# Query-key products of the second block from fp32r halves: three products in place of one full fp32 product

## The chip, the cores and the metric

The kernel runs on one core of one Trainium2 chip. The metric is the device time in microseconds (us) of one execution; lower is better. The core has five engines that matter here: PE (TensorE, matrix products), ACT (ScalarE), DVE (VectorE), POOL (GpSimd) and SP, which only issues the loads of weights. Each works through its own queue in order and waits on semaphores for the others.

## The reference

The whole computation is a model of two blocks on a sequence of 512 tokens and width 1024, all in fp32. The first block (a pooling layer, a dilated attention layer and two convolutional feed-forward layers) is not touched. The second block has two layers; each projects the normed input to seven parts and runs four "retention" heads and four "stick-breaking" heads of width 128, then an output projection and a gated feed-forward layer. What the change touches are the products of queries and keys of both kinds of head:

```
scores = jnp.einsum('bhnid,bhnjd->bhnij', qc, kc) * intra_decay[:, None]      # retention, q and k rotated
intra = jnp.einsum('bhnij,bhnje->bhnie', scores, vc)
...
z = jnp.einsum('bhtd,bhsd->bhts', qb, kb).astype(jnp.float32) * scale         # stick-breaking
valid = s_pos < t_pos
log_keep = jnp.where(valid, jax.nn.log_sigmoid(-z), 0.0)
later = lax.cumsum(log_keep, axis=3, reverse=True) - log_keep
w = jnp.where(valid, jnp.exp(jax.nn.log_sigmoid(z) + later), 0.0)
```

## The kernel before

Most matrix products of the kernel are made of fp32r halves. A value is split into a high half (ACT writes it, as a copy into an fp32r tile) and a low half (DVE subtracts the high half from the value, into another fp32r tile), and a product is then three: high by high, low by high, high by low (three(), called by gemm()). A few products still take fp32 operands whole, and among them are the keys by queries of the second block: products(), called by r1() for a retention head and by s1() for a stick-breaking head. For one head a set of products is four products, one for each block of 128 keys, that are 512, 384, 256 and 128 columns wide (only keys up to the query count); 1280 columns in all. The profile records a full fp32 product as two matmul instructions.

In each of the two layers, eight tiles of value weights come first, then 20 tiles for the heads: five for each of four head pairs x = 0 to 3, in phases ph = 0 to 4: the stick-breaking keys, its queries, the retention keys, its queries, and the gate. One tile is a gemm() of 24 matmuls. Head work is laced into this stream of tiles by hand, at fixed places on each engine:

- PE, loop over t in pe_program. For pair x: s3 of the pair before (weights by values, stick-breaking) in phase 0 after k = 3; r1 of the pair before ahead of phase 1; finish(x-1, 0), the two products that sum a head's squares for its norm, in the middle of phase 1; r2 of the pair before ahead of phase 2; in the middle of phase 2 first finish(x-1, 1) and then s1(x); in phase 4 after k = 1 the cumulative sums s2(x). After the last pair s3, r1, and then the output projection (group()), with the last finish and r2 inside.
- ACT, loop over t in act_program. prep() copies a tile of weights to its high half, two tiles ahead. In phase 2: r2 (copy of a head's output and its square), finish (Ln and Exp of the norm), s1 for the two narrow blocks (Abs, Exp, Ln), head_high, turned_pair (two copies TMP that swap the halves of the rotated keys, as soon as the tile of phase 2 is done), s1 for the two wide blocks. In phase 3 s1_high makes SPH, the high half for s2.
- DVE, loop in dve_program. prep() makes the low halves of the weights. In phase 2: square_low, finish, s1 for the narrow blocks, head_low, the rotated keys (K<-PS,RT), s1 for the wide blocks. At the head of phase 3 s1_low makes SPO, which s2 on PE reads.
- POOL multiplies TMP by the sine and adds it to K or Q. SP loads weight tiles into two RAW buffers, each after the low half of the tile that was there.

Keys and queries lie in three buffers each, K[n] and Q[n], used in turn. PE's accumulators for z are banks 2 to 4.

Of the kernel before, what the change touches and what calls it, by code (L numbers as in the profile page):

```python
# [6 lines left out]
F32 = mybir.dt.float32  # L7
# [294 lines left out]
    return n * p + sum(sets(i) for i in range(m)), (n - 4) * p + sum(sets(i) - 1 for i in range(m))  # L302


STD = {FFN1: 6, FFN2: 5, FFN3: 5}
FACTORS = {1: (((),) * 6, ((0,), (2,), (5,), (8,), (10,), ()), ((1,), (3,), (6,), (9,), (11,), ()),
               ((), (4,), (7,), (), (), ())),
# [55 lines left out]
class Core:  # L363


    def __init__(self, nc, stream, cd, colsd, xt, basd, attd, retd, out):
# [79 lines left out]
        self.G = [at(f"G{i}", 173056 + 2048 * i, 512) for i in range(2)]  # L446
        self.W = [at("WS", 177152, 2048), at("WR", 219136, 2048)]
        self.CT, self.MU = at("CT", 227328, 4), at("MU", 227392, 16)
        self.TMP = {"k": at("TMP0", 185344, 512), "q": at("TMP1", 187392, 512)}
        self.AA, self.SPL = at("AA", 189440, 1280), at("SPL", 194560, 1280)  # L450
        self.SPH, self.SPO = at("SPH", 199680, 1280, F32R), at("SPO", 204800, 1280, F32R)
# [11 lines left out]
        def sem(name):  # L463
# [2 lines left out]

        self.mix = [sem(f"mix{i}") for i in range(5)]
        self.raw, self.ara = [sem(f"raw{i}") for i in range(2)], [sem(f"ara{i}") for i in range(6)]
        self.d_c, self.d_co, self.d_bas, self.d_att, self.d_ret = (
            sem(n) for n in ("d_c", "d_co", "d_bas", "d_att", "d_ret"))  # L470
        self.d_x, self.d_out = [sem(f"d_x{i}") for i in range(4)], sem("d_out")

        self.kon, self.cond, self.ada, self.gain = sem("kon"), sem("cond"), sem("ada"), sem("gain")
# [41 lines left out]
            sem(n) for n in ("fmm", "fln", "frs", "fy", "fg", "fh", "fl"))  # L515

        self.gained, self.yd = sem("gained"), sem("yd")

        self.tv, self.th, self.tl = sem("tv"), sem("th"), sem("tl")
        self.uv, self.uh, self.ul, self.c1 = (sem(n) for n in ("uv", "uh", "ul", "c1"))  # L520
# [130 lines left out]
def pe_program(c):  # L651
# [400 lines left out]
    ffn(1, FFN1, None, (3, BANK["norm3"]))  # L1052


    def products(K, Q, order, done):

        for y in order:
            b, c0 = SBK[y]
            vacate(b)
            mm(PS[b][:, c0:c0 + WID[y]], K[:, 128 * y:128 * y + 128], Q[:, 128 * y:512],  # L1060
               y < 2 or y == (3 if order[0] else 2), True).then_inc(done, 1)

    def r1(l, x):
        h, n = 4 * l + x, (2 * x + 1) % 3
        q.wait_ge(c.rq, 2 * h + 2)
        products(c.K[n], c.Q[n], (0, 1, 2, 3), c.zr)
        for y in (0, 1, 2, 3):
            free[SBK[y][0]] = (c.rd, 4 * h + y + 1)

# [11 lines left out]

    def s1(l, x):
        h, n = 4 * l + x, 2 * x % 3
        q.wait_ge(c.sqk, 2 * h + 2)
        products(c.K[n], c.Q[n], (3, 2, 1, 0), c.zs)
        for y in (3, 2, 1, 0):
            free[SBK[y][0]] = (c.zf, 4 * h + 4 - y)

# [76 lines left out]
    for l, first, out, f, ffn0 in ((0, IN0, OUT0, 2, FFN2), (1, IN1, OUT1, 3, FFN3)):  # L1165
        value_tiles(l, first, 0)
        value_tiles(l, first + 4, 1)
        for t in range(20):
            x, ph = divmod(t, 5)
            if x and ph == 1:  # L1170
                r1(l, x - 1)
            elif x and ph == 2:
                r2(l, x - 1)

            def mid(k):
                if x and ph == 0 and k == 4:
                    s3(l, x - 1)
                elif x and ph == 1 and k == 4:
                    finish(l, x - 1, 0)
                elif ph == 2 and k == 4:  # L1180
                    if x:
                        finish(l, x - 1, 1)
                    s1(l, x)
                elif ph == 4 and k == 2:
                    s2(l, x)

            h = 4 * l + x
            freed = ((c.sqk, 2 * h + 1), (c.sqk, 2 * h + 2), (c.rot, 2 * h + 1), (c.rot, 2 * h + 2), (c.g0, h + 1))[ph]
            gemm(first + 8 + t, c.H1H, c.H1L, split(16 * l), freed, mid)
        s3(l, 3)  # L1190
        r1(l, 3)

        def mixed(k):
            return (c.fl, 8 * l + (2 * k + 2 if k < 4 else 2 * k - 7))

        def hook(n):
            if n == 3:
                finish(l, 3, 0)
                r2(l, 3)
            elif n == 8:  # L1200
                finish(l, 3, 1)

        group(out, [(c.HH, c.HL, mixed)] * 3, [(c.res, RES[out] + n + 1) for n in range(3)],
              (4, 0, 5, 1, 6, 2, 7, 3), 6, hook)
        for n in range(3, 8):
            gemm(out + n, c.HH, c.HL, mixed, (c.res, RES[out] + n + 1))
        ffn(f, ffn0, split(16 * l + 8), None, lambda k: norm(5 + 2 * l, 7) if k == 4 else None)
# [3 lines left out]
def act_program(c):  # L1211
# [108 lines left out]


    table("silu")
    nc.scalar.dma_start(c.COND[0:1, :], c.cd.rearrange("(o n) -> o n", o=1)).then_inc(c.d_c, 16)
    q.wait_ge(c.d_c, 16)
    act(c.COND[0:1, :], c.COND[0:1, :], ACT.Silu).then_inc(c.cond, 1)
    for k in range(8):
        q.wait_ge(c.d_x[k // 2], 16)
# [373 lines left out]
    def s1_high(h):  # L1701
        q.wait_ge(c.lat, 4 * h)
        for y in (3, 2, 1, 0):
            q.wait_ge(c.msk, 4 * h + 4 - y)
            act(c.SPH[:, OFF[y]:OFF[y] + WID[y]], c.SPL[:, OFF[y]:OFF[y] + WID[y]]).then_inc(c.sph, 1)

    def s2(h):
        for y in (3, 2, 1, 0):
            a = c.AA[:, OFF[y]:OFF[y] + WID[y]]
            q.wait_ge(c.laf, 4 * h + 4 - y)  # L1710
            act(a, a, ACT.Exp).then_inc(c.wex, 1)
# [56 lines left out]
    for l, first, out, f, ffn0 in ((0, IN0, OUT0, 2, FFN2), (1, IN1, OUT1, 3, FFN3)):  # L1768
# [22 lines left out]
        for t in range(20):  # L1791
            x, ph = divmod(t, 5)
            h = 4 * l + x
            if ph == 1 and x:
                gate(h - 1)
            elif ph == 3:
                s1_high(h)
            prep(first + 8 + t + 2)
            if ph == 0 and x:
                s3(h - 1)  # L1800
            elif ph == 1 and x:
                finish(h - 1, 0)
                head_high(h - 1, 0)
            elif ph == 2:
                if x:
                    r2(h - 1)
                    finish(h - 1, 1)
                s1(h, (3, 2))
                if x:
                    head_high(h - 1, 1)  # L1810
                turned_pair(t, h, 2)
                s1(h, (1, 0))
            elif ph == 3:
                turned_pair(t, h, 3)
            elif ph == 4:
                s2(h)
        prep(out + 2)
        h = 4 * l + 3
        s3(h)
        gate(h)  # L1820
        finish(h, 0)
# [33 lines left out]
def dve_program(c):  # L1855
# [523 lines left out]
    def scores(p, m):  # L2379

        u = 4 * p + m
        n, w = blocks(m)
        q.wait_ge(c.al0, 8)
        q.wait_ge(c.tr, turned(u - 1)[0] if u else 0)
        q.wait_ge(c.d_att, 16)
        for hh in range(2):
            sb = c.SB[u % 2][:, 512 * hh:512 * hh + 512]
            q.wait_ge(c.s1, 2 * u + hh + 1)
            stt(sb[:, 0:128 * n], c.ATT[:, 256 - 128 * n:256], float(SL[0][2 * p + hh]), PS[2 + hh][:, 0:128 * n],
                ALU.mult, ALU.add)  # L2390
            for g in (1, 2):
                o = 96 + 160 * g + 96 - 32 * m
                ins = stt(apart(sb, m, g), c.ATT[:, o:o + 64 * w].rearrange("p (m j) -> p m j", j=32),
                          float(SL[g][2 * p + hh]), apart(PS[2 + hh], m, g), ALU.mult, ALU.add)
            ins.then_inc(c.b4, 1)
        for hh in range(2):
            o, z = 512 * hh, 8 * (u % 2) + 4 * hh
            q.wait_ge(c.b4, 2 * u + hh + 1)
            step(nc.vector.tensor_reduce(c.STAT[:, z:z + 1], c.SB[u % 2][:, o:o + 128 * (n + w)], AX_X, ALU.max))
            nc.vector.tensor_scalar(c.STAT[:, z + 1:z + 2], c.STAT[:, z:z + 1], -1.0, None, ALU.mult  # L2400
                                    ).then_inc(c.mx, 1)
# [90 lines left out]
    def s1_low(h):  # L2492
        for y in (3, 2, 1, 0):
            o = slice(OFF[y], OFF[y] + WID[y])
            q.wait_ge(c.sph, 4 * h + 4 - y)
            tt(c.SPO[:, o], c.SPL[:, o], c.SPH[:, o].bitcast(F32), ALU.subtract).then_inc(c.spo, 1)

    def s2(h):
        def later(y):
            b, c0 = LBK[y]  # L2500
# [14 lines left out]

    def r1(h):
        q.wait_ge(c.zr, 4 * h + 4)
        q.wait_ge(c.d_ret, 16 * (h // 4 + 1))
        q.wait_ge(c.so, h + 1)
        for y in range(4):  # L2520
            b, c0 = SBK[y]
# [39 lines left out]
    for l, first, out, f, ffn0 in ((0, IN0, OUT0, 2, FFN2), (1, IN1, OUT1, 3, FFN3)):  # L2561
        for t in range(28):
            x, ph = divmod(t - 8, 5)
            h = 4 * l + x
            if t >= 8 and ph == 3:
                s1_low(h)
            prep(first + t + 2)
            if l == 0 and 2 <= t <= 9:
                stt(c.xk(t - 2), c.xk(t - 2), c.cols("final_g", t - 2), c.SS[:, :], ALU.mult, ALU.mult
                    ).then_inc(c.xs, 1)  # L2570
            if t < 8:
                if t == 1 and l == 0:
                    both()
                elif t == 5:
                    q.wait_ge(c.nrs, NORMN[7] if l else 0)
                    q.wait_ge(c.fac, 1)
                    q.wait_ge(c.d_ret, 16 * (l + 1))
                    tt(c.COS, c.COS, c.SG[:, :], ALU.mult)
                    tt(c.SIN, c.SIN, c.SG[:, :], ALU.mult).then_inc(c.turn, 1)
                elif t == 7:  # L2580
                    values_out(l, first)
                continue
            if ph == 1 and x:
                r1(h - 1)
                finish(h - 1, 0)
                head_low(h - 1, 0)
            elif ph == 2:
                if x:
                    square_low(h - 1, 1)
# [21 lines left out]
                    s1(h, (1, 0))  # L2611
            else:
                tt(c.G[h % 2][:, :], P, c.SG[:, :], ALU.mult).then_inc(c.g0, 1)
        prep(out + 2)
        h = 4 * l + 3
        square_low(h, 0)
        r1(h)
        finish(h, 0)
# [74 lines left out]
def sp_program(c):  # L2693
# [35 lines left out]
    for u in range(6, len(UNITS)):  # L2729
        load(u)  # L2730
        if after.get(u) == ATT0 + 5:
            q.wait_ge(c.al0, 8)
            nc.sync.dma_start(c.ATT[:, :], c.attd).then_inc(c.d_att, 16)
        elif u in after:
            q.wait_ge(c.mm, mm_at((IN0 if after[u] == IN0 + 5 else IN1) - 1))
            nc.sync.dma_start(c.RT[:, :], c.retd).then_inc(c.d_ret, 16)
    for part in range(2):
        for k in range(8):
            q.wait_ge(c.yd, 8 * part + k + 1)
# [50 lines left out]
```

## Time and profile before

| | |
|---|---|
| median of three runs | 2599.99 us (2599.57 to 2600.58) |
| the profiled execution | 2599.9 us, span 2597.9 us |
| granted TensorE clock, mean | 0.999 |
| PE busy | 2581.2 us, 99% of the span |
| weight loads of PE busy | 2187.6 us, 84% |
| DVE busy | 1682.2 us, 65% |
| ACT busy | 1174.9 us, 45% |
| POOL busy | 115.2 us, 4% |
| loads | 296.84 MB, mean 114 GB/s |

Busy is the time in which an engine had an instruction in work. Matmuls are pipelined: each lasts longer than the distance to the next one's start, so PE's cost has to be read from starts, not from durations or from the busy share. The stretches of the heads are about 1440 to 1597 us (first layer) and 2037 to 2193 us (second layer).

### The profile page before, as it was taken

To read this page: it belongs to the slowest core of one execution; us is meant where nothing else is said; L and a number is where in the kernel's file an instruction comes from. 1 tells how busy PE (TensorE), PEld (TensorE's weight loads), DVE (VectorE), ACT (ScalarE), POOL (GpSimd) and SP (SyncE) were. 2 spreads that over 40 slices of the span, in tenths; PEclk is the share of its full clock that TensorE was granted. 3 is DMA by queue.
4 is the path that set the end of the run, shared out by engine and by line. 5 is a ranking of instruction groups with operands and counts; after the bars stand their busy time and mean duration, and the time that the engine had idled before them with its cause. 6 is when DMAs were issued, how large, how long until landed. Compare 5 with 4: busy or idle time off the path is not lost.

```text
span 2597.9 us, 37965 instructions
## 1 busy us (share of the span) xinstructions
PE 2581.2 (99%) x15677; PEld 2187.6 (84%) x15677; DVE 1682.2 (65%) x2593; ACT 1174.9 (45%) x1802; POOL 115.2 (4%) x85
## 2 busy tenths in 40 slices
PE   9999999999999999999999999999999999999998
PEld 5788888978888888898998877898998877898997
DVE  7877777644444446884974666883874566784883
ACT  2343233543343334552753465552553466543553
POOL 0000000000000000021200010000000011000000
PEclk9999999999999999999999999999999999999999
DMA  9345755222221221223323211222323211233222
GB/s 403 139 175 206 292 194 197 72 104 81 82 82 66 82 82 66 93 90 103 114 98 126 82 65 68 84 102 99 114 97 122 91 49 65 98 109 111 92 92 86
DMA packets 46765, 296.84 MB, mean 114 GB/s; under 512 B 5121, under 2 KB 7297, under 8 KB 17410
## 3 DMA queue, kind: packets, MB, share of 16 engines
q1 hardware_dynamic: 46592, 294.42, 31.2%
q8 instruction: 124, 2.03, 0.3%
q14 instruction: 47, 0.39, 0.0%
q10 hardware_dynamic: 2, 0.00, 0.0%
HBM read 292.30 MB, written 2.10 MB: 113 GB/s over the span
## 4 chain that ended last, share of the span: by engine, by line
PE 94%; DVE 2%; ACT 2%; issue 1%; POOL 0%; DVEq 0%; POOLq 0%; ACTq 0%
PE PS L661 93%; PE PS L719 1%; ACT WH L1220 1%; DVE AA L1862 0%; DVE XT L1862 0%; DVE QLH L1862 0%; DVE QVH L1862 0%; ACT TMP L1220 0%; ACT AA L1220 0%; DVE Tb L1862 0%; DVE Yb L1865 0%; ACT H1H L1220 0%; POOL QVW L2656 0%; DVE PS L1862 0%; DVE WL L1862 0%
## 5 line engine op out<-in xcount | busy, mean ns | idle before, releaser
L1862 DVE TENSOR_TENSOR WL<-RAW,WH 128x1024 fp32r<-128x1024 f32 (+1 forms) x300 | 398.2, 1327 | 382.8 <-ACT WH L1220 380.8
L661 PE MATMUL PS<-H1H,WH 128*128 128x512 f32 (+1 forms) x1344 | 515.2, 383 | 0.4 <-DVE H1L L1862 0.4
L661 PE MATMUL PS<-H1H,WL 128*128 128x512 f32 (+1 forms) x1344 | 503.4, 375 | 0.0
L661 PE MATMUL PS<-H1L,WH 128*128 128x512 f32 (+1 forms) x1344 | 503.1, 374 | 0.0
L1220 ACT ACTIVATE WH<-RAW 128x1024 fp32r<-128x1024 f32 (+1 forms) x300 | 336.3, 1121 | 213.4 <-PE PS L661 180.3
L661 PEld LDWEIGHTS PS<-H1H,WH 128*128 128x128 f32 x1344 | 253.1, 188 | 51.2 <-issue 5.4
L661 PEld LDWEIGHTS PS<-H1L,WH 128*128 128x128 f32 x1344 | 253.2, 188 | 47.4 <-issue 4.1
L661 PEld LDWEIGHTS PS<-H1H,WL 128*128 128x128 f32 x1344 | 252.9, 188 | 45.7
L661 PE MATMUL PS<-H2Hb,WH 128*128 128x512 f32 (+1 forms) x408 | 160.9, 394 | 0.0
L661 PE MATMUL PS<-H2Lb,WH 128*128 128x512 f32 (+1 forms) x408 | 154.3, 378 | 0.0
L661 PE MATMUL PS<-H2Hb,WL 128*128 128x512 f32 (+1 forms) x408 | 154.3, 378 | 0.0
L661 PE MATMUL PS<-TH,QHH 128*128 128x256 f32 x504 | 142.8, 283 | 2.1 <-ACT KEPT L1220 2.1
L661 PE MATMUL PS<-TL,QHH 128*128 128x256 f32 x504 | 142.6, 283 | 0.0
L661 PE MATMUL PS<-GHd,WH 128*128 128x512 f32 (+1 forms) x374 | 141.1, 377 | 0.0
L661 PE MATMUL PS<-GLd,WH 128*128 128x512 f32 (+1 forms) x374 | 140.9, 377 | 0.0
L661 PE MATMUL PS<-GHd,WL 128*128 128x512 f32 (+1 forms) x374 | 140.8, 377 | 0.0
L1885 DVE CUSTOM_DVE_ANT_0 AR<-AR,COND,CO 128x1024 f32<-128x1024 f32 x112 | 138.9, 1281 | 1.9 <-DMA AR<-stream 1.5
L661 PE MATMUL PS<-TH,QLH 128*128 128x256 f32 x432 | 122.2, 283 | 0.0
L661 PE MATMUL PS<-TH,QHW 128*128 128x256 f32 x392 | 110.9, 283 | 0.0
L661 PE MATMUL PS<-TL,QHW 128*128 128x256 f32 x392 | 110.9, 283 | 0.0
L661 PEld LDWEIGHTS PS<-TH,QHH 128*128 128x128 f32 x504 | 96.7, 192 | 2.6 <-ACT KEPT L1220 2.5
L1220 ACT ACTIVATE KEPT<-PS 128x256 f32<-128x256 f32 x200 | 75.6, 378 | 48.6 <-PE PS L661 43.4
(372 smaller groups left out, 5544.1 us busy)
## 6 DMA issues: line engine op xcount, KB each, us to landing
RAW<-stream SPq DMA_DIRECT2D x169, 1024.0 KB, 4.8
AR<-stream SPq DMA_DIRECT2D x56, 1024.0 KB, 8.1
RAW<-stream SPq DMA_DIRECT2D x64, 704.0 KB, 4.0
RT<-ret SPq DMA_DIRECT2D x2, 1536.0 KB, 6.6
MIX<-stream SPq DMA_DIRECT2D x4, 640.0 KB, 16.3
XT<-xt SPq DMA_DIRECT2D x4, 512.0 KB, 5.5
y<-XT SPq DMA_DIRECT2D x16, 128.0 KB, 1.8
MIX<-stream SPq DMA_DIRECT2D x1, 1024.0 KB, 16.5
```

Of the source, the lines that this page charges most:

```text
L661: return nc.tensor.matmul(out, weights, moving, start=start, stop=stop, skip_group_check=True)
L719: ins = nc.tensor.transpose(PS[b][:, 128 * n:128 * n + 128], block, c.IDENT)
L1220: return nc.scalar.activation(out, src, fn, **kw)
L1862: return nc.vector.tensor_tensor(out, a, b, op)
L1885: ins = nc.vector.tensor_tensor_reduce(src, src, c.COND[:, :], 1.0, bias, ALU.mult, ALU.add, c.mod(col, 1))
```

## The change

products() takes halves: for each key block the high keys by the high queries, the high keys by the low queries, and the low keys by the high queries. ACT makes the high halves and DVE the low ones, in new steps at fixed places of their loops; the low halves are written over K[n] and Q[n]. On PE s1(x) now stands ahead of finish(x-1, 1). On DVE r1 of the pair before moves ahead of prep() in phase 1, and head_low(x-1, 0) from phase 1 to the head of phase 2. Three DMA semaphores for tables and the one for the condition vector become one, with matching counts. Cut to its core:

```
+        self.KLO = [at(f"KLO{i}", 160768 + 2048 * i, 512, F32R) for i in (3, 4, 5)]
+        self.QLO = [at(f"QLO{i}", 160768 + 2048 * i, 512, F32R) for i in (0, 1, 2)]
+        self.KQR = at("KQR", 194560, 1024, F32R)
...
-    def products(K, Q, order, done):
+    def products(KH, KL, QH, QL, order, done):
...
-            mm(PS[b][:, c0:c0 + WID[y]], K[:, 128 * y:128 * y + 128], Q[:, 128 * y:512],
-               y < 2 or y == (3 if order[0] else 2), True).then_inc(done, 1)
+            out, keys = PS[b][:, c0:c0 + WID[y]], slice(128 * y, 128 * y + 128)
+            mm(out, KH[:, keys], QH[:, 128 * y:512], y < 2 or y == (3 if order[0] else 2), False)
+            mm(out, KH[:, keys], QL[:, 128 * y:512], False, False)
+            mm(out, KL[:, keys], QH[:, 128 * y:512], False, True).then_inc(done, 1)
...
     def r1(l, x):
         h, n = 4 * l + x, (2 * x + 1) % 3
-        q.wait_ge(c.rq, 2 * h + 2)
-        products(c.K[n], c.Q[n], (0, 1, 2, 3), c.zr)
+        q.wait_ge(c.hel, HALF[l, "qr", x])
+        products(c.KQR[:, 0:512], c.KLO[n][:, :], c.KQR[:, 512:1024], c.QLO[n][:, :], (0, 1, 2, 3), c.zr)
...
-        q.wait_ge(c.sqk, 2 * h + 2)
-        products(c.K[n], c.Q[n], (3, 2, 1, 0), c.zs)
+        q.wait_ge(c.hel, HALF[l, "qs", x])
+        products(chunk(c.HL, 3), c.KLO[n][:, :], chunk(c.HL, 7), c.QLO[n][:, :], (3, 2, 1, 0), c.zs)
...
                 elif ph == 2 and k == 4:
+                    s1(l, x)
                     if x:
                         finish(l, x - 1, 1)
-                    s1(l, x)
...
+    def scaled_high(h):
+
+        KH, n = chunk(c.HL, 3), 2 * (h % 4) % 3
+        q.wait_ge(c.sqk, 2 * h + 1)
+        act(KH, c.K[n][:, :]).then_inc(c.heh, 1)
+
+    def queries_high(h):
+
+        QH, n = chunk(c.HL, 7), 2 * (h % 4) % 3
+        q.wait_ge(c.sqk, 2 * h + 2)
+        act(QH, c.Q[n][:, :]).then_inc(c.heh, 1)
+
+    def turned_high(h):
+
+        n = (2 * (h % 4) + 1) % 3
+        q.wait_ge(c.spo, 4 * h + 4)
+        q.wait_ge(c.rq, 2 * h + 1)
+        act(c.KQR[:, 0:512], c.K[n][:, :]).then_inc(c.heh, 1)
+        q.wait_ge(c.rq, 2 * h + 2)
+        act(c.KQR[:, 512:1024], c.Q[n][:, :]).then_inc(c.heh, 1)
...
+            elif ph == 2:
+                queries_high(h)
             elif ph == 3:
                 s1_high(h)
             prep(first + 8 + t + 2)
-            if ph == 0 and x:
-                s3(h - 1)
-            elif ph == 1 and x:
-                finish(h - 1, 0)
-                head_high(h - 1, 0)
+            if ph == 0:
+                if x:
+                    turned_high(h - 1)
+                    s3(h - 1)
+            elif ph == 1:
+                scaled_high(h)
+                if x:
+                    finish(h - 1, 0)
+                    head_high(h - 1, 0)
...
+        h = 4 * l + 3
+        turned_high(h)
         prep(out + 2)
-        h = 4 * l + 3
         s3(h)
...
+    def queries_low(h):
+
+        QH, n = chunk(c.HL, 7), 2 * (h % 4) % 3
+        q.wait_ge(c.heh, HALF[h // 4, "qs", h % 4])
+        tt(c.QLO[n][:, :], c.Q[n][:, :], QH.bitcast(F32), ALU.subtract).then_inc(c.hel, 1)
...
+            if t >= 8 and ph == 1 and x:
+                r1(h - 1)
+            elif t >= 8 and ph == 2:
+                if x:
+                    head_low(h - 1, 0)
+                queries_low(h)
             prep(first + t + 2)
...
-            if ph == 1 and x:
-                r1(h - 1)
-                finish(h - 1, 0)
-                head_low(h - 1, 0)
+            if ph == 0 and x:
+                turned_low(h - 1)
+            elif ph == 1:
+                if x:
+                    finish(h - 1, 0)
+                keys_low(h)
...
+        h = 4 * l + 3
+        turned_low(h)
         prep(out + 2)
```

keys_low() is made like queries_low(), and turned_low() does the same for the two rotated tiles. KLO and QLO are the addresses of K and Q under an fp32r type; KQR lies on part of SPL.

## Rows read from the trace of the kernel before

**Rows 1.** The page, part 4: shares of the chain by engine.
```profile
PE 94%; DVE 2%; ACT 2%; issue 1%; POOL 0%; DVEq 0%; POOLq 0%; ACTq 0%
```
**Rows 2.** Busy time of each engine, heads of the first layer: us, then busy (count).
```profile
1440.00:1600.00 160.00, 159.45 (x705) 125.25 (x704) 107.89 (x191) 97.21 (x162) 23.93 (x16) 1.00 0.19 68
```
**Rows 3.** The tile K on PE: ns min/median/max, first and last start.
```profile
L661 PE MATMUL PS<-Q,K x128: 270/434/592, 1452.8 to 2193.0; 128*128 128x128 f32 x32, 128*128 128x256 f32 x32, 128*128 128x384 f32 x32, 128*128 128x512 f32 x32
```
**Rows 4.** Timeline of PE, pairs 0 and 1: start us, duration us, instruction, count.
```profile
1452.79 2.32 PE L661 MATMUL PS<-Q,K 128*128 128x128 f32 x8
...
1479.31 2.32 PE L661 MATMUL PS<-Q,K 128*128 128x512 f32 x8
...
1481.69 0.39 PE L661 MATMUL PS<-H1L,WH 128*128 128x512 f32 x1
...
1492.52 0.39 PE L661 MATMUL PS<-OSL,KR 128*128 128x512 f32 x1
1492.75 2.32 PE L661 MATMUL PS<-Q,K 128*128 128x128 f32 x8
```
**Rows 5.** Timeline of PE, cumulative sums s2 of pair 1.
```profile
1504.24 0.39 PE L661 MATMUL PS<-H1H,WL 128*128 128x512 f32 x1
...
1504.66 0.30 PE L661 MATMUL PS<-SPH,KR 128*128 128x128 f32 x1
1504.79 0.28 PE L661 MATMUL PS<-SPO,KR 128*128 128x128 f32 x1
1504.90 0.27 PE L661 MATMUL PS<-SPH,KR 128*128 128x128 f32 x1
...
1506.05 0.34 PE L661 MATMUL PS<-SPO,KR 128*128 128x384 f32 x1
1506.23 0.22 PE L661 MATMUL PS<-SPH,KR 128*128 128x128 f32 x1
```
**Rows 6.** Timeline of PE, a run of fp32r products 256 columns wide.
```profile
2297.02 0.28 PE L661 MATMUL PS<-TL,QHG 128*128 128x256 f32 x1
2297.14 0.28 PE L661 MATMUL PS<-TH,QLG 128*128 128x256 f32 x1
```
**Rows 7.** Timeline of ACT, pairs 0 and 1; in brackets idle time before it.
```profile
1457.92 1.21 ACT L1220 ACTIVATE TMP<-PS 64x512 f32<-64x512 f32 x2 [2.24 <-PE PS L661]
...
1490.37 0.64 ACT L1220 ACTIVATE OSH<-OB 128x512 fp32r<-128x512 f32 x1
1492.94 0.69 ACT L1220 ACTIVATE OC<-PS,KON 128x512 f32<-128x512 f32 x1 [1.94 <-PE PS L661]
...
1496.12 0.61 ACT L1220 ACTIVATE H2Hc<-OB 128x512 fp32r<-128x512 f32 x1
1497.87 1.21 ACT L1220 ACTIVATE TMP<-PS 64x512 f32<-64x512 f32 x2 [1.14 <-PE PS L661]
```
**Rows 8.** Timeline of DVE, pairs 0 and 1.
```profile
1450.27 0.69 DVE L1865 SCALAR_TENSOR_TENSOR Q<-PS,SG 128x512 f32<-128x512 f32 x1 [2.46 <-PE PS L661]
...
1488.31 0.68 DVE L1865 SCALAR_TENSOR_TENSOR Q<-PS,SG 128x512 f32<-128x512 f32 x1
...
1497.70 0.68 DVE L1862 TENSOR_TENSOR H2Lc<-OB,H2Hc 128x512 fp32r<-128x512 f32 x1
...
1504.02 0.29 DVE L1862 TENSOR_TENSOR SPL<-SPL,BAS 128x128 f32<-128x128 f32 x1
1504.22 1.69 DVE L1862 TENSOR_TENSOR SPO<-SPL,SPH 128x128 fp32r<-128x128 f32 x4
```
**Rows 9.** Timeline of ACT, end of the first layer's heads.
```profile
1592.12 0.63 ACT L1220 ACTIVATE AA<-AA 128x512 f32<-128x512 f32 x1 [0.28 <-DVE AA L1862]
1592.65 1.04 ACT L1220 ACTIVATE WH<-RAW 128x1024 fp32r<-128x1024 f32 x1
```
**Rows 10.** Timelines of DVE and PE there.
```profile
1592.99 0.68 DVE L1862 TENSOR_TENSOR G<-PS,SG 128x512 f32<-128x512 f32 x1
...
1594.40 2.32 PE L661 MATMUL PS<-Q,K 128*128 128x512 f32 x8
```

More of the change, by code:

```diff
@@ L302, in turned, with head_halves @@
     return n * p + sum(sets(i) for i in range(m)), (n - 4) * p + sum(sets(i) - 1 for i in range(m))
+def head_halves():
+    order = []
+    for l in range(2):
+        for x in range(4):
+            if x:
+                order += [(l, "kr", x - 1), (l, "qr", x - 1)]
+            order += [(l, "ks", x), (l, "qs", x)]
+        order += [(l, "kr", 3), (l, "qr", 3)]
+    return {key: n + 1 for n, key in enumerate(order)}
+HALF = head_halves()
 STD = {FFN1: 6, FFN2: 5, FFN3: 5}
@@ L468, in __init__ @@
         self.raw, self.ara = [sem(f"raw{i}") for i in range(2)], [sem(f"ara{i}") for i in range(6)]
-        self.d_c, self.d_co, self.d_bas, self.d_att, self.d_ret = (
-            sem(n) for n in ("d_c", "d_co", "d_bas", "d_att", "d_ret"))
+        self.d_tab, self.d_co, self.d_bas = (sem(n) for n in ("d_tab", "d_co", "d_bas"))
         self.d_x, self.d_out = [sem(f"d_x{i}") for i in range(4)], sem("d_out")
@@ L517, in __init__ @@
         self.gained, self.yd = sem("gained"), sem("yd")
+        self.heh, self.hel = sem("heh"), sem("hel")
         self.tv, self.th, self.tl = sem("tv"), sem("th"), sem("tl")
@@ L1322, in act_program @@
     table("silu")
-    nc.scalar.dma_start(c.COND[0:1, :], c.cd.rearrange("(o n) -> o n", o=1)).then_inc(c.d_c, 16)
-    q.wait_ge(c.d_c, 16)
+    nc.scalar.dma_start(c.COND[0:1, :], c.cd.rearrange("(o n) -> o n", o=1)).then_inc(c.d_tab, 16)
+    q.wait_ge(c.d_tab, 16)
     act(c.COND[0:1, :], c.COND[0:1, :], ACT.Silu).then_inc(c.cond, 1)
@@ L2384, in scores @@
         q.wait_ge(c.tr, turned(u - 1)[0] if u else 0)
-        q.wait_ge(c.d_att, 16)
+        q.wait_ge(c.d_tab, 32)
         for hh in range(2):
@@ L2496, in s1_low, with keys_low, turned_low @@
             tt(c.SPO[:, o], c.SPL[:, o], c.SPH[:, o].bitcast(F32), ALU.subtract).then_inc(c.spo, 1)
+    def keys_low(h):
+        KH, n = chunk(c.HL, 3), 2 * (h % 4) % 3
+        q.wait_ge(c.heh, HALF[h // 4, "ks", h % 4])
+        tt(c.KLO[n][:, :], c.K[n][:, :], KH.bitcast(F32), ALU.subtract).then_inc(c.hel, 1)
+    def queries_low(h):
+        QH, n = chunk(c.HL, 7), 2 * (h % 4) % 3
+        q.wait_ge(c.heh, HALF[h // 4, "qs", h % 4])
+        tt(c.QLO[n][:, :], c.Q[n][:, :], QH.bitcast(F32), ALU.subtract).then_inc(c.hel, 1)
+    def turned_low(h):
+        n = (2 * (h % 4) + 1) % 3
+        q.wait_ge(c.heh, HALF[h // 4, "kr", h % 4])
+        tt(c.KLO[n][:, :], c.K[n][:, :], c.KQR[:, 0:512].bitcast(F32), ALU.subtract).then_inc(c.hel, 1)
+        q.wait_ge(c.heh, HALF[h // 4, "qr", h % 4])
+        tt(c.QLO[n][:, :], c.Q[n][:, :], c.KQR[:, 512:1024].bitcast(F32), ALU.subtract).then_inc(c.hel, 1)
     def s2(h):
@@ L2517, in r1 @@
         q.wait_ge(c.zr, 4 * h + 4)
-        q.wait_ge(c.d_ret, 16 * (h // 4 + 1))
+        q.wait_ge(c.d_tab, 48 + 16 * (h // 4))
         q.wait_ge(c.so, h + 1)
@@ L2576, in dve_program @@
                     q.wait_ge(c.fac, 1)
-                    q.wait_ge(c.d_ret, 16 * (l + 1))
+                    q.wait_ge(c.d_tab, 48 + 16 * l)
                     tt(c.COS, c.COS, c.SG[:, :], ALU.mult)
@@ L2582, in dve_program @@
                 continue
-            if ph == 1 and x:
-                r1(h - 1)
-                finish(h - 1, 0)
-                head_low(h - 1, 0)
+            if ph == 0 and x:
+                turned_low(h - 1)
+            elif ph == 1:
+                if x:
+                    finish(h - 1, 0)
+                keys_low(h)
             elif ph == 2:
@@ L2613, in dve_program @@
                 tt(c.G[h % 2][:, :], P, c.SG[:, :], ALU.mult).then_inc(c.g0, 1)
+        h = 4 * l + 3
+        turned_low(h)
         prep(out + 2)
-        h = 4 * l + 3
         square_low(h, 0)
@@ L2732, in sp_program @@
             q.wait_ge(c.al0, 8)
-            nc.sync.dma_start(c.ATT[:, :], c.attd).then_inc(c.d_att, 16)
+            nc.sync.dma_start(c.ATT[:, :], c.attd).then_inc(c.d_tab, 16)
         elif u in after:
             q.wait_ge(c.mm, mm_at((IN0 if after[u] == IN0 + 5 else IN1) - 1))
-            nc.sync.dma_start(c.RT[:, :], c.retd).then_inc(c.d_ret, 16)
+            nc.sync.dma_start(c.RT[:, :], c.retd).then_inc(c.d_tab, 16)
     for part in range(2):
```

## The prediction

> **What bounds the kernel now.** I read the chain of waits first: 94% of it is PE [rows 1]. The busy times of the stretch of heads say the same, 159.45 of 160 us for PE against 107.89 for DVE and 97.21 for ACT [rows 2] (columns: length, PE, PEld, DVE, ACT, POOL, clock, DMA share, GB/s). The clock was 1.00 there, the upper of its two levels. So PE's own products count at once, and so does every wait put into its queue.
>
> But a matmul's duration overlaps the next one's, so a short wait of PE can hide inside "busy". Hence the timelines, where only starts are read. In pair 1, the last product ahead of the cumulative sums starts at 1504.24; a 512-wide product has its follower 0.23 later (1492.52 to 1492.75, [rows 4]), so s2 could start at 1504.47. It starts at 1504.66 [rows 5]. DVE's first SPO subtraction starts at 1504.22 and a 128-wide one lasts 0.29 [rows 8], so its result was there at 1504.51, and PE started 0.15 later. **PE waits 0.19 us for DVE there**, in each pair. That chain begins at the copies TMP, for which ACT sat idle 1.14 us until the tile of phase 2 was done [rows 7]: from 1497.87 to 1504.66 is 6.79 us, nearly what PE needs for its 30 products in between (30 x 0.23 = 6.9). Whatever makes ACT late for TMP by more than 1.14 us makes PE wait at s2.
>
> **The products.** There are 16 sets (8 pairs, r1 and s1 each), 128 recorded instructions of 8 a set [rows 3]. One set costs 2.15 us: r1 starts at 1479.31, and the second product of the next tile starts at 1481.69, one step of 0.23 behind the first [rows 4]. The new set is twelve fp32r products, three of each width. Steps from start to start: 512 wide 0.23 [rows 4]; 384 wide 0.18, 128 wide 0.11 (1506.05 to 1506.23 and 1504.79 to 1504.90, [rows 5]); 256 wide 0.12 [rows 6]. So 3 x (0.23 + 0.18 + 0.12 + 0.11) = 1.92 us, a gain of 0.23 a set. Call this r. Its lower bound is columns alone at the pace of wide products, 3840/512 x 0.23 = 1.72; the upper one is no gain, 2.15. I take 1.92, since every width has its own row. That 256 columns take hardly longer than 128 shows that below 256 it is something other than columns that sets the pace.
>
> The Trainium skill (TensorE: Matmul & The Clock Gate, LDWEIGHTS) puts a load of 128 weight columns at 128/1.2 = 107 ns, and this speaks against the change, which needs twelve loads of its own per set. The trace agrees for the narrow ones (0.11 and 0.12). By the page's figures, with 213 and 160 ns for the two wide blocks (same page, Back-to-back issue gap) and 107 for the two narrow ones, a set would be 1.76 us, an estimate; the sum goes by the rows' 1.92.
>
> **The halves.** A 512-wide fp32r write costs ACT 0.64 [rows 7] and a 512-wide subtraction DVE 0.68 [rows 8]. Four of each per pair, 16 of each in a layer: 10 us of ACT and 11 us of DVE, which have 63 and 52 us free in the first layer's heads [rows 2]. They cost only where someone waits.
> - Stick-breaking keys, and all rotated halves but the last pair's: they fall where ACT and DVE idle ahead of the next tile's end. Nothing.
> - Stick-breaking queries: Q is scaled at 1488.31 [rows 8]; one write, head_low (0.7) and the subtraction end by about 1490.4, and s1 is due at 1492.1 (1492.75 less finish's two steps of 0.23, less 0.23). Nothing. In pair 0 of each layer it is close: Q at 1450.27, ready 1450.96, halves by 1452.5, plus 0.15, against s1 at 1452.79 [rows 8, 4]. Nothing, or 0.2.
> - Weight preparation on both engines slips by about 1 us in phase 2; the tile is used two tiles (over 10 us) later. Nothing, and the loads behind it neither. DVE's r1 ahead of prep() frees the scores sooner; no one waits for them.
> - **The last pair of a layer has no cover**: r1 follows s3 directly. ACT writes K's half from 1592.65 (where WH now starts, after a step of 0.53), Q's from 1593.18, ended 1593.82 [rows 9]. DVE starts G at 1592.99 [rows 10], K's low half at 1593.6 and Q's at 1594.2, ended 1594.9; PE 0.15 later, 1595.05. r1 started at 1594.40 [rows 10]: **+0.65 per layer**. What follows on ACT and DVE slips by up to 1 us against slack at least that large.
>
> **s1 ahead of finish** (pairs 1 to 3 of both layers, where there is a pair before). The norm's Ln on ACT began at 1492.94 [rows 7]. PE now reaches this place 2.15 - r earlier (r1) but does s1 first: Ln at 1492.94 - (2.15 - r) + r, for r = 1.92 1494.63. From Ln to the start of H2Hc ACT works through Exp and s1's narrow blocks without a gap, 3.18 us, and H2Hc takes a step of 0.53 [rows 7, 9]. So TMP can start at 1494.63 + 3.71 = 1498.34, 0.47 later than before. PE by then is 0.46 earlier. The 1.14 us of idle are eaten and the chain of 6.79 us starts late: s2 starts 0.47 later than before and PE's wait of 0.19 becomes 1.12. DVE keeps up: H2Lc, moved from 1497.70 by 1.69, ends at 1500.1, and the rotated K after it at 1500.8, while ACT is still at the wide blocks, 1.2 us of TMP and four steps behind. In general the pair comes out 2r - 3.37 us later than before; the savings of r1 and s1 are inside that. Pair 0 has no finish, and TMP there had 2.24 us of idle [rows 7]: it keeps its gain, 2.15 - r = 0.23.
>
> **The sum** per layer: -0.23 + 3 x 0.47 + (0.65 - 0.23) = +1.6 us; two layers **+3.2 us**. On the profiled execution's 2599.9 us that is **2603.1**; it stands 0.1 under the median of the runs shown, so nothing is shifted. In general the change is 16r - 27.5: 0.0 us at r = 1.72, +6.9 at 2.15. A change under 0.2% (5.2 us) can't be told from none here.
>
> **The rivals.**
> - *Cheap products*, a set at the pace of its columns, r = 1.72: the sum is 0.0, 2599.9. For: loads can run ahead under wide products. Against: 128 columns took 0.11 and not 0.06. Chance 0.20. The Trainium skill's load of weights (same page and section), with its 1.76, would make it 16 x 1.76 - 27.5 = +0.7, 2600.6, an estimate.
> - *Slower beyond doubt: the sets gain nothing.* Place: the twelve products with their own loads and the change of kind of weights on both sides; price r = 2.15, so PE is no earlier and finish a full 2.15 late: +6.9, 2606.8. It decides from r = 2.04 on, where the sum passes 5.2. For: no row shows a run whose widths and weight tiles change as these do, and it needs only 0.02 us more for each of the twelve. Against: steps of one width repeat to 0.01. Chance 0.17, with further waits of the kind "s1 for the queries' low half" in it.
> - *Faster: the chain doesn't hold.* If s2's 0.19 is a start-up gap and ACT takes its steps denser than I lay them out, PE keeps all savings: with r = 1.72, 16 x 0.43 = 6.9 less 1.3 for the layers' ends, -5.6, 2594.3. Against: 0.15 us from SPO's end to s2's start is what a hand-over costs, and leaves nothing for a start-up. Chance 0.06.
> - *The change isn't what it says*: three products of full cost, 16 x 4.3 = +69 us and more. The rows of fp32r products exclude it, at 0.23 for 512 columns. Chance 0.01.
>
> **How the numbers follow.** Forecast 0.56. Within 0.2%: the forecast, the cheap products = 0.76. Slower: 0.17 + 0.01 = 0.18. Faster: 0.06. The range, 2598.8 to 2607.0, takes in the two bounds of r, about 1 us below the lower for slack I priced too high; it leaves out the faster rival, the last one and some of the waits.
>
> **What would show it.** In the profile after: a set at 1.9 us from start to start; ACT with no idle time ahead of TMP in pairs 1 to 3 (1.14 before), and PE's gap ahead of the SPH products at 1.3 to 1.4 us instead of 0.42, with the wait now named; pair 0 unchanged at about 0.42; r1 after the last s3 about 0.65 late, behind DVE. The period of a pair, 39.96 between the starts of two s1 before [rows 4], longer by about 0.5. Wrong: TMP still preceded by idle time in pairs 1 to 3, a wait of PE at s1, or a gap at s2 that isn't longer.

## The result and the profile after

The changed kernel takes **2603.89 us** (median of 20 runs, 2603.34 to 2604.32), the kernel before 2600.06 (20 runs on the same chip): a ratio of 1.0015, 95% interval 1.0009 to 1.0021, so 3.8 us slower. Forecast were 2603.1 and +3.2 us. The profiled execution has a span of 2601.8 us against 2597.9.

The page's first and fourth parts, of the kernel after (the shares of [rows 1] were 94, 2 and 2%):

```profile
PE 2577.4 (99%) x15741; PEld 2194.3 (84%) x15741; DVE 1700.0 (65%) x2625; ACT 1191.2 (46%) x1834; POOL 116.5 (4%) x85
PE 92%; ACT 4%; DVE 3%; issue 1%; POOL 0%; DVEq 0%; POOLq 0%; ACTq 0%
```

PE is busy for less time than before (2581.2), and the program is longer: two points of the chain went over to ACT and one to DVE. Busy time by engine for the stretch of [rows 2], after:

```profile
1440.00:1600.00 160.00, 155.79 (x730) 127.07 (x729) 116.66 (x206) 104.92 (x177) 24.52 (x16) 1.00 0.19 67
```

PE had 0.5 us of idle there and now has 4.2. PE's timeline of pair 1 shows where, first in one set of products (r1), then at the point ahead of s2 that answers to [rows 5]. A step is the distance from one start to the next:

```profile
1479.07 0.39 PE L678 MATMUL PS<-KQR 128*128 128x512 f32 x1
1479.29 0.39 PE L678 MATMUL PS<-QLO,KQR 128*128 128x512 f32 x1
1479.52 0.39 PE L678 MATMUL PS<-KQR,KLO 128*128 128x512 f32 x1
1479.75 0.33 PE L678 MATMUL PS<-KQR 128*128 128x384 f32 x1
...
1480.27 0.29 PE L678 MATMUL PS<-KQR 128*128 128x256 f32 x1
...
1480.64 0.22 PE L678 MATMUL PS<-KQR 128*128 128x128 f32 x1
...
1483.71 0.39 PE L678 MATMUL PS<-OSH,KR 128*128 128x512 f32 x1
...
1503.47 0.39 PE L678 MATMUL PS<-H1H,WL 128*128 128x512 f32 x1
1504.97 0.30 PE L678 MATMUL PS<-SPH,KR 128*128 128x128 f32 x1 [1.12 <-DVE SPO L1909]
```

From r1's first product to OSH are 4.64 us, of which 12 products of a tile take 2.73 (12 steps of 0.2275); the set costs 1.91. The three blocks of 512, 384 and 256 columns took 0.68, 0.52 and 0.37. In the kernel before, OSH follows r1's first product (1479.31, [rows 4]) after 4.90 us:

```profile
1484.21 0.39 PE L661 MATMUL PS<-OSH,KR 128*128 128x512 f32 x1
```

Read in the same way a set cost 2.17 us there, so the new set saves 0.26.

The step ahead of the SPH product is 1.50, with the wait now named: 1.12 us for DVE's SPO. It was 0.42. The named wait is counted from the modelled end of the product before it (0.39 us long), not from the 0.23 after which a follower could start; counted from there PE waits 1.27 us, and it waited 0.19.

What makes SPO late stands in ACT's timeline of the same pair, to be laid beside [rows 7]:

```profile
1494.35 0.69 ACT L1239 ACTIVATE OC<-PS,KON 128x512 f32<-128x512 f32 x1 [3.82 <-PE PS L678]
1495.07 0.63 ACT L1239 ACTIVATE OC<-OC 128x512 f32<-128x512 f32 x1
1495.61 0.53 ACT L1239 ACTIVATE AA<-PS 128x128 f32<-128x128 f32 x2
...
1497.54 0.62 ACT L1239 ACTIVATE H2Hc<-OB 128x512 fp32r<-128x512 f32 x1
1498.18 1.22 ACT L1239 ACTIVATE TMP<-PS 64x512 f32<-64x512 f32 x2
```

ACT sits idle for 3.82 us until finish's products are there, then works without a gap up to TMP: the 1.14 us of idle time ahead of TMP have gone. The next pair's first SPH product is at 1545.47, so the period of a pair (from one first SPH product to the next) is 40.50 us; it was 39.95.

The end of the first layer's heads, PE and DVE, answers to [rows 10]:

```profile
1593.56 2.42 PE L678 MATMUL PS<-AA,WS 128*128 128x128 f32 x8 [0.47 <-DVE AA L1909]
1596.35 0.50 PE L678 MATMUL PS<-KQR 128*128 128x512 f32 x1 [0.37 <-DVE QLO L1909]
```

From s3's start to r1's is 2.79 us here and was 2.26: r1 waits for the queries' low half.

### The profile page after: what moved, and what is told of

The parts are those of the page before. It is cut to its first block, busy times and chain, and to the rows that moved or that the text cites. A ratio compares the mean times of both kernels' runs of the same rounds, so it can differ in the third digit from the quotient of the medians.

```text
span 2601.8 us, 38159 instructions
## 1 busy us (share of the span) xinstructions
PE 2577.4 (99%) x15741; PEld 2194.3 (84%) x15741; DVE 1700.0 (65%) x2625; ACT 1191.2 (46%) x1834; POOL 116.5 (4%) x85
## 3 DMA queue, kind: packets, MB, share of 16 engines
q8 instruction: 125, 2.05, 0.3%
## 4 chain that ended last, share of the span: by engine, by line
PE 92%; ACT 4%; DVE 3%; issue 1%; POOL 0%; DVEq 0%; POOLq 0%; ACTq 0%
PE PS L678 91%; PE PS L736 1%; ACT AA L1239 1%; ACT WH L1239 1%; DVE AA L1909 0%; ACT TMP L1239 0%; ACT OC L1239 0%; DVE SPL L1912 0%; DVE XT L1909 0%; DVE QLH L1909 0%; DVE Tb L1909 0%; DVE Yb L1912 0%; ACT H1H L1239 0%; POOL QVW L2732 0%; DVE QVH L1909 0%
```

## The experiments

Two theories beside each other. A: the halves are nearly free, the products gain 0.24 us a set, and the loss is the place of finish behind s1 in PE's queue, with the layer's end as the second cost. B: it is the work on the halves that makes ACT and DVE late for s2. The expectations name a third, C: the fp32r sets themselves save nothing; e1 against e3 tests it. Each group of kernels was timed beside the kernel before on its chip (2599.77 for e1 to e4, 2599.50 for e5 to e7, 2600.29 for e8 and e9). The differences are at most 0.25% of the time, and of the intervals of e1 to e9 only those of e2, e4 and e9 exclude 1. So the causes rest on the steps in the traces, which repeat from pair to pair within 0.03 us.

**e1, finish first.** The changed kernel with

```
                 elif ph == 2 and k == 4:
-                    s1(l, x)
                     if x:
                         finish(l, x - 1, 1)
+                    s1(l, x)
```

> The changed kernel with finish(x-1, 1) ahead of s1(x) on PE again; all else as in the change. Theory A (the order costs): each of the six pairs that have a pair before gets back 0.93 to 1.03 us, PE's gap ahead of the SPH products falls from 1.50 to about 0.42 in them, and ACT is idle again ahead of TMP; span about 2595.7, time 2597.5, some 6 us under the changed kernel and 2.6 under the kernel before. Theory B (the halves' work on ACT and DVE makes s2 late, in whichever order PE goes): the gap stays near 1.5 and the time at 2603 to 2604. Theory C (the fp32r sets bring nothing and the rest comes from them): about 2603.9 as well.

2597.74 us, ratio to before 0.9992 (0.9983 to 1.0001): 2.0 us under the kernel before; the interval just takes in 1, though the slowest of its runs (2598.74) lies under the fastest of before (2599.04). The period of a pair is 39.53 us, 0.97 less than in the changed kernel, six times 5.8 us. Its timelines of PE and of ACT:

```profile
1492.62 0.39 PE L678 MATMUL PS<-OSH,KR 128*128 128x512 f32 x1
1492.85 0.50 PE L678 MATMUL PS<-OSL,KR 128*128 128x512 f32 x1
1493.19 0.22 PE L678 MATMUL PS<-H2Lc 128*128 128x128 f32 x1
...
1504.41 0.39 PE L678 MATMUL PS<-H1H,WL 128*128 128x512 f32 x1
1504.83 0.30 PE L678 MATMUL PS<-SPH,KR 128*128 128x128 f32 x1
```
```profile
1493.39 0.69 ACT L1239 ACTIVATE OC<-PS,KON 128x512 f32<-128x512 f32 x1 [2.02 <-PE PS L678]
1498.04 1.21 ACT L1239 ACTIVATE TMP<-PS 64x512 f32<-64x512 f32 x2 [0.86 <-PE PS L678]
```

The step at s2 is 0.42 again, and ACT is idle ahead of TMP. All halves are still made. That is theory A's reading and not B's. The third line is s1's first product, 0.34 us behind OSL's; in the kernel before it followed after 0.23 [rows 4]. e3 and e6 take this up.

**e2, the swap alone**, the reverse edit in the kernel before: s1 ahead of finish, full fp32 products, no halves.

> The kernel before with only the order on PE changed: s1(x) ahead of finish(x-1, 1), products still full fp32, no halves. Theory A: ACT reaches TMP 0.93 us too late in six pairs, PE's gap ahead of the SPH products is about 1.35 instead of 0.42, +5.6 us, time 2605.6. Theories B and C: no more than 0.5 us from 2600.1, since no halves are made.

2606.23 us, ratio 1.0024 (1.0015 to 1.0034), +6.5 us. PE in pair 1:

```profile
1504.86 0.39 PE L661 MATMUL PS<-H1H,WL 128*128 128x512 f32 x1
1506.35 0.30 PE L661 MATMUL PS<-SPH,KR 128*128 128x128 f32 x1 [1.10 <-DVE SPO L1862]
```

A wait named at 1.10 us without any half being made, and a pair of 41.03 us against 39.95: 1.08 for the swap. The swap alone costs more than the whole change.

**e3, halves made but unused.** On top of e1 the products read whole K and Q, and the low halves go to tiles that nothing reads; the computation's result stays that of full fp32 products.

```
-            mm(out, KH[:, keys], QH[:, 128 * y:512], y < 2 or y == (3 if order[0] else 2), False)
-            mm(out, KH[:, keys], QL[:, 128 * y:512], False, False)
-            mm(out, KL[:, keys], QH[:, 128 * y:512], False, True).then_inc(done, 1)
+            mm(out, KL[:, keys], QL[:, 128 * y:512], y < 2 or y == (3 if order[0] else 2), True).then_inc(done, 1)
...
-        tt(c.QLO[n][:, :], c.Q[n][:, :], QH.bitcast(F32), ALU.subtract).then_inc(c.hel, 1)
+        tt(chunk(c.HH, 7), c.Q[n][:, :], QH.bitcast(F32), ALU.subtract).then_inc(c.hel, 1)
```

> As e1 (finish first), and all halves are made on ACT and DVE at the same places and with the same waits, but the low halves go to tiles that nothing reads, and products() multiplies whole fp32 keys by queries as before. Theory A: the halves alone cost only at the end of each layer, 0.54 each: 2601.2. Theory B: 2 to 6 us over the kernel before, with a gap of over 1 us ahead of the SPH products. Theory C: 2600 to 2601 and e1 no faster than this one; by theory A e1 is faster than this one by 16 x 0.24 = 3.8 us.

2601.82 us, ratio 1.0008 (0.9999 to 1.0017), +2.05 us: the halves' own price. The step at s2 is 0.41, so it isn't paid there. It is paid at the ends of the layers (s3 to r1 2.79 us, twice 0.53) and at a place that the prediction had not: OSL's product is followed after 0.33 to 0.34 instead of 0.23 us, six times 0.11. A longer wait of PE in the first layer's feed-forward part (for the tile KEPT, which ACT writes; 1.40 us instead of 1.05) adds about 0.35. e1 is 4.1 us under e3 with three fp32r products in place of one full one, 16 sets of 0.25, which answers theory C.

**e4, the layers' ends covered.** On top of e1, for the last pair ACT writes the rotated keys' high half ahead of s2, and DVE makes both low halves ahead of the gate's tile.

```
             elif ph == 4:
+                if x == 3:
+                    turned_keys(h)
                 s2(h)
...
             elif ph == 4:
                 s2(h)
+                if x == 3:
+                    turned_low(h)
             P = PS[BANK[first + t]][:, :]
```

> As e1, and for the last pair of a layer ACT writes the rotated keys' high half ahead of its s2 instead of behind it, and DVE makes both low halves ahead of the gate's tile instead of behind it. Theory A: r1 follows s3 without a wait (2.26 us from start to start as before, 2.79 in the changed kernel), 0.5 a layer: 1.1 us under e1, 2596.4. Rival: s3 or something behind it gets late by as much, no change against e1.

2596.42 us, ratio 0.9988 (0.9979 to 0.9997). It is 1.3 us under e1. From s3 to r1 are 2.20 us (2.26 in the kernel before), with no wait named: 0.59 less than in e1 at each of the two layers' ends, which explains the 1.3 but for 0.1.

**e5, the wide blocks first.** On top of e4, in phase 2 s1(h, (1, 0)) goes ahead of turned_pair() on ACT and ahead of the rotated keys on DVE.

> As e4, and in phase 2 ACT takes s1's wide blocks ahead of TMP, DVE its own wide blocks ahead of the rotated keys, so that s2's chain no longer starts at the end of the tile of phase 2. Theory A (that chain is what PE waits for at s2, 0.19 us in each of eight pairs): the gap ahead of the SPH products falls from 0.42 to 0.23, 1.5 us under e4, 2594.9. Rival: the 0.42 is a start-up gap of the first SPH product and stays: 2596.4; or TMP, now 3 us later, frees its bank too late for the tile of phase 4: slower.

2598.77 us: 2.6 us over e4, each against its own runs of before, where 1.5 us under it were expected. The first SPH product does follow after 0.22, so the 0.19 us of wait at s2 was real, but the rival that the expectation named came true: PE now waits for the bank of the rotated keys' tile.

```profile
1502.00 0.39 PE L678 MATMUL PS<-H1H,WL 128*128 128x512 f32 x1
1502.83 0.47 PE L678 MATMUL PS<-H1H,WH 128*128 128x512 f32 x1 [0.44 <-DVE K L1917]
```

The step is 0.83 instead of 0.23: 0.60 lost, and the same wait stands in all six pairs that have a pair before. Why DVE is late there is told in the last section.

**e6, OSL early**, on top of e5: square_low(h - 1, 1) ahead of prep() in phase 2 on DVE.

> As e5, and DVE makes OSL (square_low of the pair before) ahead of the weights' low half in phase 2. In e1 and e3 the step from OSL's product to the next was 0.33 to 0.34 us instead of 0.23: read as a wait for OSL, which the query's low half and the later weight copy push back. Theory A: the step returns to 0.23 in six pairs, 0.6 us under e5, 2594.3. Rival: the step belongs to the change of operands: same as e5.

2598.21 us, 0.6 us less than e5. The runs of the two overlap, but the period of a pair fell from 39.99 to 39.86 us and the step after OSL's product is 0.23: the 0.11 us was a wait, and it belongs to the halves, which push OSL back.

**e7, ACT and DVE follow PE's new order.** The changed kernel with its own order on PE; on ACT and DVE s1's narrow blocks stand ahead of finish, and head_high and head_low behind s1's wide blocks.

```
                 if x:
                     r2(h - 1)
-                    finish(h - 1, 1)
                 s1(h, (3, 2))
                 if x:
-                    head_high(h - 1, 1)
+                    finish(h - 1, 1)
                 turned_pair(t, h, 2)
                 s1(h, (1, 0))
+                if x:
+                    head_high(h - 1, 1)
```

> The changed kernel with its own order on PE (s1 ahead of finish), but ACT and DVE take s1's narrow blocks ahead of finish(x-1, 1), and head_high and head_low of that head go behind s1's wide blocks. Theory A, sharpened (the swap costs only because ACT's queue holds s1's narrow blocks, head_high and TMP behind finish's Ln): ACT is idle ahead of TMP again, the gap at s2 0.42, time as e1, 2597.5 to 2598. If finish coming late on PE costs by itself (OSH, OC and the norm holding something else): 2601 or more, near the changed kernel's 2603.9.

2599.56 us, the same as before (ratio 1.0001): about 2 us more than expected. ACT and PE in pair 1:

```profile
1496.31 1.21 ACT L1239 ACTIVATE TMP<-PS 64x512 f32<-64x512 f32 x2 [1.15 <-PE PS L678]
```
```profile
1502.68 0.39 PE L678 MATMUL PS<-H1H,WL 128*128 128x512 f32 x1
1503.69 0.30 PE L678 MATMUL PS<-SPH,KR 128*128 128x128 f32 x1 [0.62 <-DVE SPO L1910]
```

ACT is on time, 1.15 us idle ahead of TMP, and PE still waits for SPO, with a step of 1.01. DVE shows why: the low half of the retention head stood between the last mask and the first SPO.

```profile
1502.45 0.29 DVE L1910 TENSOR_TENSOR SPL<-SPL,BAS 128x128 f32<-128x128 f32 x1
1502.66 0.69 DVE L1910 TENSOR_TENSOR H2Lc<-OB,H2Hc 128x512 fp32r<-128x512 f32 x1
1503.26 1.69 DVE L1910 TENSOR_TENSOR SPO<-SPL,SPH 128x128 fp32r<-128x128 f32 x4
```

**e8, that low half behind s1_low**, all else as e7.

> As e7, and DVE's head_low of the retention head goes behind s1_low instead of ahead of it. In e7 ACT was idle 1.15 us ahead of TMP again, but PE's gap at s2 was 1.01: read as head_low's 0.60 us standing between DVE's last mask and its first SPO. Theory A: the gap falls to 0.42, 6 x 0.45 = 2.7 us under e7, 2596.9, so that the change's own order on PE costs nothing once both other queues follow it. Rival: the gap stays near 1, the late finish on PE holds something else.

2597.69 us, ratio 0.9991 (0.9982 to 1.0000), 2.6 us under before; the pair takes 39.42 us and the step at s2 is 0.41:

```profile
1503.08 0.39 PE L678 MATMUL PS<-H1H,WL 128*128 128x512 f32 x1
1503.49 0.30 PE L678 MATMUL PS<-SPH,KR 128*128 128x128 f32 x1
```

The changed kernel's pair is 1.08 us longer, as much as the swap cost in e2. So the change's order on PE costs nothing by itself. It cost a microsecond a pair because the queues of ACT and DVE kept the old order.

**e9, the narrowest block early.** e4 with OSL early as in e6, and SPH and SPO of the 128-column block made in phase 2, in idle time.

```
                     head_high(h - 1, 1)
+                s1_high(h, (3,))
                 turned_pair(t, h, 2)
...
                     head_low(h - 1, 1)
+                s1_low(h, (3,))
```

> As e4 (finish first, both ends of the layers covered), with OSL ahead of the weights' low half, and with the high and low half of s1's narrowest block (SPH and SPO of 128 columns) made in phase 2, in the idle time ahead of TMP and ahead of the rotated keys. Theory A: OSL's step is 0.23 and the gap ahead of the first SPH product falls from 0.42 to 0.23: 6 x 0.11 + 8 x 0.19 = 2.2 us under e4, 2594.3. Rival (the gap is a start-up of that product): 2595.8. Worse if the two small steps push TMP or the rotated keys.

**2594.15 us**, ratio 0.9977 (0.9968 to 0.9986): 6.1 us under the kernel before and nearly 10 under the changed one. Its PE at the place of [rows 5]:

```profile
1502.97 0.39 PE L678 MATMUL PS<-H1H,WL 128*128 128x512 f32 x1
1503.20 0.22 PE L678 MATMUL PS<-SPH,KR 128*128 128x128 f32 x1
```

The step is a plain 0.23 and the pair 39.15 us. The three losses found in a pair are gone: 1.08 for the swap and 0.19 at s2, and 0.11 behind OSL's product. That the step at s2 falls to 0.23 also shows that the 0.19 was a wait and no start-up gap of the first SPH product.

## Why the prediction was right

The mechanism held at each place that the prediction priced. +3.2 us were forecast and +3.8 measured. Part of that closeness is luck: in the swap and at the layers' ends, errors in opposite directions partly cancelled.

- *The set.* 1.91 us was measured against 1.92 forecast from the steps of each width. The rivals with r = 1.72 and r = 2.15 fall. But the 2.15 before was read too early: the tile behind a set starts a little slower (some of its steps are 0.24 and not 0.2275), and read up to OSH a set cost 2.17. The gain is 0.26 a set and not 0.23; e1 against e3 gives 0.25 by the time of the runs, and a pair of e8 is 0.53 shorter than before. The estimate of 1.76 us from the Trainium skill (TensorE: Matmul & The Clock Gate, LDWEIGHTS) was too low: 256 columns took 0.12 each and not 0.107, 384 columns 0.17 and not 0.160, 512 columns 0.2275 and not 0.213. For the wide blocks the Trainium skill (same page, Back-to-back issue gap) adds 2.5 ns to the columns' time, which the prediction left out; with it the estimate is 1.78, still too low.
- *s1 ahead of finish.* The mechanism is shown by undoing it (e1), by doing it alone (e2) and by moving the other two queues after it (e7, e8). The swap was priced at 0.93 us a pair (0.47 later where 0.46 would have been gained) and measured at 1.08, by e2 against before and by the changed kernel against e8. e1 gives 0.97 only because it carries the 0.11 behind OSL. Against the 1.08 stand two sets of 0.26, so a pair came out 0.55 longer and not 0.47; both terms were too small, and the difference hides half of it. From the start of H2Hc to TMP ACT took 0.64 us, not 0.53, while PE brought finish 0.04 earlier than forecast; from TMP to s2 were 6.79 us, exactly as before. Six pairs make 0.5 us, most of what the forecast lacked. The step at s2 is 1.50 and not the forecast's 1.3 to 1.4. That the profile's 1.12 us of wait equals the 1.12 in the prediction is chance: the prediction counts from the 0.23 step, and so counted it is 1.27.
- *The layer's end.* 0.65 us of wait were forecast, 0.53 measured. ACT and DVE did their steps when forecast, but PE started 0.05 us behind the end of QLO (1595.61 + 0.69 on DVE, 1596.35 on PE) and not 0.15. The first product there had a step of 0.34, as it has in e4 without a wait (0.33), and r1's gain was 0.15 us only; the net, +0.38, is close to the +0.42 of the sum because the two errors nearly cancel.
- *Pair 0.* Its first SPH product came at 1464.46 and before at 1464.70: 0.24 earlier where 0.23 was forecast, and no wait at s1, where the forecast had left 0 to 0.2.
- *Halves elsewhere at nothing.* Right in the heads of the changed kernel, where finish is late anyway, but only there: with finish first they delay OSL by 0.11 us in each of six pairs (e1, e3), a price that the prediction did not look for.
- The rival that the chain doesn't hold and the one that the change isn't what it says are excluded by the wait for SPO and by the steps of the products.

Left open: the span grew by 3.9 us, the heads account for 3.6. About 0.3 stand in the first layer's feed-forward part behind them, where a wait of PE for KEPT lasts 1.40 us and lasted 1.05. It is 1.40 in e1, e3 and e8 too, and 1.05 in e2, which is later there than the changed kernel but makes no halves. So it isn't the shift; it comes with the halves or with another of the change's edits, and nothing was tried on it.

## What to carry to other kernels

When work is moved up in one engine's queue, ask what now stands behind the thing that it passed, on every engine that consumes it: here the consumer's queue had the old order, and moving s1 up made everything late that ACT does after finish. Cost a swap by the chain of the other queues from that point to their next meeting, not by what the moved step itself gains. And on an engine that is 99% busy, read starts, not busy shares: the 0.19 us in each pair that showed PE already at the end of this chain was in no list of waits.

## What the runs showed that was not expected

In e5 DVE's mask on 128 columns lasted 1.16 us instead of 0.29, and the four SPO subtractions 2.80 instead of 1.69. DVE's and POOL's timelines:

```profile
1500.92 1.16 DVE L1917 TENSOR_TENSOR SPL<-SPL,BAS 128x128 f32<-128x128 f32 x1
1502.01 0.68 DVE L1917 TENSOR_TENSOR K<-PS,RT 128x512 f32<-128x512 f32 x1
1502.61 2.80 DVE L1917 TENSOR_TENSOR SPO<-SPL,SPH 128x128 fp32r<-128x128 f32 x4
```
```profile
1500.64 1.29 POOL L2740 TENSOR_TENSOR TMP<-TMP,RT 128x512 f32<-128x512 f32 x1 [30.45 <-ACT TMP L1239]
1502.76 1.29 POOL L2740 TENSOR_TENSOR K<-K,TMP 128x512 f32<-128x512 f32 x1 [0.83 <-DVE K L1917]
```

The long mask lies over POOL's multiplication and ends just after it (1502.08, POOL 1501.93); POOL's addition falls into the four subtractions, which the view shows as one group. K<-PS,RT, with one input in PSUM, kept its 0.68. The Trainium skill (SBUF — State Buffer, SBUF: two separate sides) has this as a port pair shared by DVE and GpSimd, held for a whole instruction, when the DVE instruction has two SBUF inputs and the GpSimd one reads SBUF; the trace agrees. In the kernel before, DVE's steps beside POOL's two in phase 2 have one input in PSUM or DVE is idle; moving TMP put the mask and the SPO beside them.

This also changes what e5 says. The mask's usual 0.29 in place of 1.16 would have let K<-PS,RT begin 0.87 us earlier and free its bank at about 1501.8. With the 0.14 us from K's end (1502.69) to PE's start (1502.83), PE could have gone on at about 1501.96, and it was due only at 1502.23 (1502.00 and a step of 0.23). By this estimate the bank alone would have cost nothing, and the 0.60 us of wait came from the port. No run tried the order of e5 without POOL beside the mask.
